# A hybrid attention and RWKV-7 trunk: head norms, rotary turn and forget gates moved from a stage of their own into the RWKV scan, and a new order of work in the forgetting attention

## The reference, cut to what matters

```python
def _hybrid_layer(x, pos, ...):
    h = _rmsnorm(x, norm_g)
    proj = h @ w_in
    (fq, fk, fv, ff, fg, r_pre, rg, sq, sk, sv, sg, cb, cc, cx, cg) = _split(proj, IN_COLS)
    y_fox = _fox_attention(_heads(fq), _heads(fk), _heads(fv), ff, fox_b_f, fox_q_norm, fox_k_norm)
    y_rwkv = _rwkv7_time_mix(r_pre, ...)
    y_swa = _swa_attention(_heads(sq), _heads(sk), _heads(sv), swa_sinks, swa_q_norm, swa_k_norm, pos)
    y_conv = _short_conv(cb, cc, cx, conv_w)
    mixed = jnp.concatenate([y_fox * silu(fg), y_rwkv * silu(rg), y_swa * silu(sg), y_conv * silu(cg)], axis=-1)
    return x + mixed @ w_out

def _fox_attention(q, k, v, f_logit, b_f, q_norm, k_norm):
    q, k = _rmsnorm(q, q_norm), _rmsnorm(k, k_norm)
    log_f = jax.nn.log_sigmoid((f_logit + b_f).astype(jnp.float32))
    Ft = jnp.cumsum(log_f, axis=1)
    # score = q.k * scale + F[query] - F[key], causal, softmax, times v

def _swa_attention(q, k, v, sinks, q_norm, k_norm, pos):
    q = _rope(_rmsnorm(q, q_norm), pos)
    k = _rope(_rmsnorm(k, k_norm), pos)
    # sliding window with sinks
```

## Time and profile before

| | us |
|---|---|
| median of 3 runs | 3686.85 (3685.52 to 3697.97) |
| profiled execution | 3691.14 |
| its span, first to last instruction | 3689.3 |
| PE busy | 3284.0 (89%) |
| DVE busy | 1552.2 (42%) |
| ACT busy | 1009.4 (27%) |
| POOL busy | 545.5 (15%) |
| mean granted PE clock | 0.916 of full |

### The profile page before, as it was taken

How to read it: one execution, slowest core, us unless ns; L and a number is a source line. 1 busy time by engine, 2 the same in 40 slices (tenths; PEclk the granted TensorE clock), 3 DMA queues, 4 the chain that set the end, 5 groups by cost and what they waited for, 6 DMA issues and landing times. The chain is left out here.

```text
span 3689.3 us, 62205 instructions
## 1 busy us (share of the span) xinstructions
PE 3284.0 (89%) x24708; PEld 2331.3 (63%) x24708; DVE 1552.2 (42%) x2258; ACT 1009.4 (27%) x1876; POOL 545.5 (15%) x304
## 2 busy tenths in 40 slices
PE   6979989999997688959979799899999976889599
PEld 4868767777774344437748687677777743444387
DVE  4127622222223565557441376222222235655575
ACT  4014312222223134333240143122222231343332
POOL 4100000000000112332241000000000001122322
PEclk9989999999998578979979899899999985788799
DMA  3225422222223310066332254222222233100663
GB/s 118 74 70 174 142 74 66 80 66 65 64 66 120 116 29 18 9 187 209 120 110 74 70 174 144 73 64 80 68 65 64 66 120 116 29 18 9 187 203 123
DMA packets 357723, 343.29 MB, mean 93 GB/s; under 512 B 95388, under 2 KB 290972, under 8 KB 353592
## 3 DMA queue, kind: packets, MB, share of 16 engines
q1 hardware_dynamic: 288520, 298.53, 25.5%
q10 hardware_dynamic: 68928, 40.93, 4.2%
HBM read 208.46 MB, written 130.91 MB: 92 GB/s over the span
## 5 line engine op out<-in xcount | busy, mean ns | idle before, releaser
L124 PE MATMUL rs_acc<-h_hi,rs_w_hi 128*128 128x512 f32 x1024 | 428.4, 418 | 0.0
L128 PE MATMUL rs_acc<-h_lo,rs_w_hi 128*128 128x512 f32 x1024 | 417.8, 408 | 0.0
L130 PE MATMUL rs_acc<-h_hi,rs_w_lo 128*128 128x512 f32 x1024 | 414.5, 405 | 0.0
L110 POOL TENSOR_TENSOR rs_w_lo<-rs_raw,rs_w_hi 128x1024 fp32r<-128x1024 f32 x32 | 76.3, 2386 | 1235.8 <-POOLq L109 1235.8
L124 PE MATMUL rp_acc<-h_hi,rp_w_hi 128*128 128x512 f32 x512 | 206.0, 402 | 41.7 <-PEq L121 41.7
L1372 ACT ACTIVATE fx_prob<-fx_ST 128x512 f32<-128x512 f32 (+3 forms) x320 | 157.2, 531 | 290.7 <-PE fx_ST L1242 150.8
L1658 PE MATMUL so_acc<-so_wo_hi,so_m_hi 128*128 128x512 f32 x512 | 209.3, 409 | 29.9 <-POOL so_m_lo L1580 25.2
L124 PEld LDWEIGHTS rs_acc<-h_hi,rs_w_hi 128*128 128x128 f32 x1024 | 192.2, 188 | 55.1 <-issue 16.5
L130 PEld LDWEIGHTS rs_acc<-h_hi,rs_w_lo 128*128 128x128 f32 x1024 | 192.6, 188 | 43.2
L128 PEld LDWEIGHTS rs_acc<-h_lo,rs_w_hi 128*128 128x128 f32 x1024 | 192.7, 188 | 36.7
L124 PE MATMUL pj_acc<-h_hi,pj_w_hi 128*128 128x512 f32 (+1 forms) x512 | 207.4, 405 | 5.3 <-PEq L121 5.3
(11 more groups left out here) (256 smaller groups left out, 6006.6 us busy)
## 6 DMA issues: line engine op xcount, KB each, us to landing
projT<-rs_stage SPq DMA_DIRECT2D x128, 256.0 KB, 2.1
pj_xb<-x SPq DMA_DIRECT2D x32, 512.0 KB, 3.3
projT<-rp_stage SPq DMA_DIRECT2D x64, 256.0 KB, 3.1
rs_raw<-w_in ACTq DMA_DIRECT2D x32, 512.0 KB
rs_nat<-rw SPq DMA_DIRECT2D x128, 128.0 KB, 2.4
so_stage<-x SPq DMA_DIRECT2D x64, 256.0 KB, 2.9
rp_pre<-projT SPq DMA_DIRECT2D x16, 899.5 KB, 8.3
projT<-pj_stage SPq DMA_DIRECT2D x56, 256.0 KB, 2.0
```

What stands on the lines that cost most here:

```text
L110: self.nc.gpsimd.tensor_tensor(self.w_lo[q][:, :, 0:m], self.raw[:, :, 0:m], self.w_hi[q][:, :, 0:m].bitcast(F32), ALU.subtract).then_inc( ...
L124: ins = M(acc, self.w_hi[q][:, k, 0:m], self.h_hi[:, k, cols], start=(k == 0), stop=False)
L128: M(acc, self.w_hi[q][:, k, 0:m], self.h_lo[:, k, cols], start=False, stop=False)
L130: ins = M(acc, self.w_lo[q][:, k, 0:m], self.h_hi[:, k, cols], start=False, stop=(k == KC - 1))
```

## The change

The head norm stage is dropped. Its work is cut into 56 units (seven blocks by eight ranges of 256 tokens), four in each of the first 14 tiles of the scan. A unit's squares are made by ACT, summed by head with one matmul on PE (`bones`, float32, 256 columns), the inverse root is taken by ACT (`factor`: Ln, then Exp), and POOL multiplies (`scale`). The 32 units of the forgetting attention come first (tiles 0 to 7); the 24 units with the turn follow (tiles 8 to 13): they also need the rows with halves of heads swapped, which SP loads by four transfers, and a block of cosines and sines. Loads and stores of the units go into SP's order between the stores of the projection (`beside`). The gates are made in tiles 0 to 7, 256 tokens each. `bt`, `kt` and `nat` of the scan lose their second buffer, so that the loads of tile `t+1` wait for `nb_free`, and the swapped rows and the cosines (`qp`, `cs`) have one buffer only.

In `phase_fox` the plan is paced: one or two `s` after each `m` (3 for 2 up to the 24th, then 19 for 20) regardless of the round, with seven of the second round's and first round's ahead of the first `m`; `r` is cut into four pieces; both heads' maxima go through one turn of four transposes in place of two of four; the evacuation `o` moves from DVE to ACT; `prob` has four buffers in place of three.

```diff
-        phase_head_norm(nc, l, projT, par, consts, rope, fa)
...
-        bt, kt = ([P.sb(f"{n}{e}", [128, NH, 64]) for e in two] for n in ("bt", "kt"))
-        nat = [P.sb(f"nat{e}", [128, 4, 2, 128]) for e in two]
+        bt, kt = P.sb("bt", [128, NH, 64]), P.sb("kt", [128, NH, 64])
+        nat = P.sb("nat", [128, 4, 2, 128])
...
+            sp.dma_start(bones[:], consts[:, 256:384]).then_inc(s["c_in"], 16)
+            sp.dma_start(gain[:], lay(par, l)[:, C_GN:C_GN + 7]).then_inc(s["c_in"], 16)
+            for a in range(0, 128, 32):
+                sp.dma_start(gainp[a ^ 32:(a ^ 32) + 32, :], lay(par, l)[a:a + 32, C_GN + 4:C_GN + 7]).then_inc(s["c_in"], 16)
+            sp.dma_start(bf[:], lay(par, l)[0:NH, C_BF - 1:C_BF + 1]).then_inc(s["c_in"], 16)
+
+            def load_norm(u):
+                e, (r, b) = u % 2, norms[u]
+                row, cols = row_of[r], slice(PAD + b * UB, PAD + (b + 1) * UB)
+                if u > 1:
+                    sp.wait_ge(q_st[e], 16 * (u // 2))
+                sp.dma_start(qx[e][:], projT[row:row + 128, cols]).then_inc(q_in[e], 16)
+                if turned(u):
+                    sp.wait_ge(s["q_out"], u)
...
+                    for a in range(0, 128, 32):
+                        sp.dma_start(qp[a ^ 32:(a ^ 32) + 32, :], projT[row + a:row + a + 32, cols]).then_inc(q_in[e], 16)
+                    sp.dma_start(cs[:], rope.rearrange("p (k t) -> p k t", k=2)[:, :, b * UB:(b + 1) * UB]).then_inc(q_in[e], 16)
+
+            def store_norm(u):
+                e, (r, b) = u % 2, norms[u]
+                sp.wait_ge(s["q_out"], u + 1)
+                sp.dma_start(projT[row_of[r]:row_of[r] + 128, PAD + b * UB:PAD + (b + 1) * UB], qx[e][:]).then_inc(q_st[e], 16)
...
+            def beside(t, b):
+                u = UT * t + b
+                if u < NU:
+                    store_norm(u)
+                    if b == 2 and t < NF:
+                        store_gates(t)
+                        if t + 1 < NF:
+                            load_gates(t + 1)
+                    if u + 2 < NU:
+                        load_norm(u + 2)
...
                     J.sp_store(sp, row, b)
+                    for i in ((0, 1), (2,), (3,), ())[b]:
+                        beside(t, i)
...
+            def scale(u):
+                e, r = u % 2, norms[u][0]
+                pool.wait_ge(s["q_sq"], u + 1)
+                G.tensor_scalar(qx[e][:], qx[e][:], gain[:, r:r + 1], None, ALU.mult)
+                if turned(u):
+                    G.tensor_scalar(qp[:], qp[:], gainp[:, r - 4:r - 3], None, ALU.mult)
+                pool.drain()
+                pool.wait_ge(s["q_fac"], u + 1)
+                G.tensor_tensor(qx[e][:], qx[e][:], qr[:], ALU.mult)
+                if turned(u):
+                    G.tensor_tensor(qp[:], qp[:], qr[:], ALU.mult)
+                    pool.drain()
+                    G.tensor_tensor(qx[e][:], qx[e][:], cs[:, 0, :], ALU.mult)
+                    G.tensor_tensor(qp[:], qp[:], cs[:, 1, :], ALU.mult)
+                    pool.drain()
+                    G.tensor_tensor(qx[e][:], qx[e][:], qp[:], ALU.add)
+                pool.drain().then_inc(s["q_out"], 1)
...
+            for t in range(NT):
...
+                for i, u in enumerate(here(t)):
...
+                    if i == 1 and t + 1 < NT:
+                        J.pool_weights(pool, (t + 1) % 2)
+                    scale(u)
...
+            def norm_sum(t, i):
+                u = UT * t + i
+                if u < NU:
+                    pe.wait_ge(s["q_sq"], u + 1)
+                    if u > 0:
+                        pe.wait_ge(s["q_fac"], u)
+                    M(bk[:, 5, UB:2 * UB], bones[:], qs[:], start=True, stop=True).then_inc(s["q_sum"], 1)
...
                 fill("p2")
+                norm_sum(t, 0)
...
                 fill("s5")
+                norm_sum(t, 1)
...
                     fill(f2)
+                    if f2 == "s7":
+                        norm_sum(t, 2)
...
                 fill("g")
+                norm_sum(t, 3)
...
+            def square(t, i):
+                u = UT * t + i
+                if u < NU:
+                    act.wait_ge(q_in[u % 2], loads[u])
+                    if u > 0:
+                        act.wait_ge(s["q_sum"], u)
+                    A(qs[:], qx[u % 2][:], ACT.Square).then_inc(s["q_sq"], 1)
...
                 evac("s3")
+                factor(t, 0)
...
                 evac("s4")
+                square(t, 1)
                 evac("s5")
...
                     evac(f1)
+                    factor(t, 1 if f1 == "s6" else 2)
+                    if f1 == "s6":
+                        square(t, 2)
                     evac(f2)
                 evac("wz")
+                square(t, 3)
                 evac("g")
+                factor(t, 3)
```

In `square`, `loads[u]` counts all transfers of a unit, for a turned one the six of its rows, its swapped rows and its cosines. In `phase_fox` the new part of the plan is:

```diff
-        NP = 3
+        NP = 4
...
-        LS = P.sb("LS", [128, 2 * QT, KX])
+        LS = P.sb("LS", [128, QT, KX])
...
+            for R in range(NR):
+                for j in range(keys[R % NQ]):
+                    turned(nm)
                     order.append(("m", R, j))
...
+                    goal = len(stat[0]) + 3 + min(nm, 24) * 3 // 2 + max(0, nm - 24) * 19 // 20
...
-                    for h in two:
-                        pe.wait_ge(s["lt_free"], lt_n[k, R, h] - 1)
-                        for j in range(QT):
-                            ins = Tr(LT[0:KX, j * 128:(j + 1) * 128], LS[:, QT * h + j, :], ident[:])
-                        ins.then_inc(s["lt_rdy"], 1)
+                    pe.wait_ge(s["lt_free"], lt_n[k, R] - 1)
+                    for j in range(QT):
+                        ins = Tr(LT[0:KX, j * 128:(j + 1) * 128], LS[:, j, :], ident[:])
+                    ins.then_inc(s["lt_rdy"], 1)
...
+                if k == "o":
+                    act.wait_ge(s["pv_done"], last[R])
...
+                    A(yo[:, R % 2], O[:], ACT.Copy).then_inc(s["o_free"], 1)
```

More of the change, by code:

```diff
@@ L594, in phase_rwkv_scan, with turned, here @@
         bk = P.ps("bk", [128, 6, 512])
+        UB = 256
+        bones = P.sb("bones", [128, 128])
+        qx = [P.sb(f"qx{e}", [128, UB]) for e in two]
+        qp, qs, qr = (P.sb(n, [128, UB]) for n in ("qp", "qs", "qr"))
+        cs = P.sb("cs", [128, 2, UB])
+        gain, gainp, eps = P.sb("gain", [128, 7]), P.sb("gainp", [128, 3]), P.sb("eps", [128, 1])
+        bf, one, carry = P.sb("bf", [NH, 2]), P.sb("one", [NH, 1]), P.sb("carry", [NH, 1])
+        ff, fg, fc = qp[0:NH, :], cs[0:NH, 0, :], cs[0:NH, 1, :]
+        norms = [(r, b) for r in range(4) for b in range(T // UB)] + [(4 + r, b) for r in range(3) for b in range(T // UB)]
+        row_of = [0, 128, 256, 384, R_SQ, R_SQ + 128, R_SK]
+        UT = 4
+        NU, NF = len(norms), T // UB
+        def turned(u):
+            return norms[u][0] > 3
+        def here(t):
+            return range(UT * t, min(UT * (t + 1), NU))
+        loads = [sum(96 if turned(i) else 16 for i in range(u % 2, u + 1, 2)) for u in range(NU)]
         J = Projector(P, nc, l, w_in, h_hi, h_lo, projT)
@@ L732, in body @@
                     take(pe, s[rdy])
+                    if c and here(t):
+                        pe.wait_ge(s["q_fac"], here(t)[-1] + 1)
                     a = (2, 0)[c]
@@ new lines, in plan, with ahead @@
+            turns, order, done, ns, nm = [], [], 0, 0, 0
+            total = sum(len(stat[R % NQ]) for R in range(NR))
+            def ahead(goal):
+                nonlocal done, ns
+                while done < len(beside) and (ns < goal or beside[done][0] == "x"):
+                    order.append(beside[done])
+                    ns += beside[done][0] == "s"
+                    if beside[done][0] == "x":
+                        turns.append((nm + 1, ("l", beside[done][1], 0)))
+                    done += 1
@@ L1099, in plan @@
+                    for r in range(1, NR):
+                        if nm >= sum(keys[i % NQ] for i in range(r)) - 2:
+                            goal = max(goal, sum(len(stat[i % NQ]) for i in range(r + 1)))
+                    ahead(min(total, goal))
             return order + [("o", NR - 1, 0), ("u", NR - 1, 0)]
@@ L1103, in phase_fox @@
         for k, R, x in order:
-            for h in (two if k == "l" else (0,) if k in "vu" else ()):
-                lt_n[k, R, h] = len(lt_n) + 1
+            if k in "lvu":
+                lt_n[k, R] = len(lt_n) + 1
         tiles = [(R, j) for R in range(NR) for j in range(keys[R % NQ])]
```

350 lines of the change are left out of this document (155 added, 195 removed).

## The result

The changed kernel takes 3738.11 us (median of 4 runs, 3735.56 to 3747.57) against 3688.83 before on the same chip: a ratio of 1.0134, 95% interval [1.0108, 1.0161]. It is slower by 1.3%. I had said 3647, a range of 3560 to 3728, and a chance of 0.17 for slower: wrong in direction, and outside the range. The profiled execution took 3735.56 (span 3733.8).

A forecast was written before the change was run, and what follows sets the result against it. Scan bound by PE's stream, norms by latencies, attention by waits and low-clock matmuls. From 3691: -220 stage removed, +8 start, +48 plain tiles, +204 turned tiles, -80 attention = 3651, as a median 3647; range 3560 to 3728.

The forecast's parts named there:

- Plain tiles: Scan tiles 0 to 7: sums 1.8 us plus PE standing 1.2 at the third unit's late square; +48 in all.
- Turned tiles: Scan tiles 8 to 13: PE's stands, sums and lower clock add 17.0 us a tile, +204 in all.
- Step 2: Turned tile: SP, held until POOL finishes, issues five transfers, landed 18.6; unit 1's square waits, PE stands 3.6 us.
- Steps 3 and 4: Turned tile: POOL's work and SP's queue with twelve loads land unit 2's transfers at 33.9; PE stands 10.2 us.
- Step 5: Turned tile, unit 3: the loop from square to square takes some 12 us, PE's work about 11; PE stands 1.
- the clock's term of 0.4: Turned tile: PE restarting at the lower level after a long stand loses 0.4 us a tile.
- POOL beside DVE: Scan: DVE's four two-input SBUF operations stand where POOL is idle, cost nothing; +24 us if that cover is gone.
- (b): Attention: pacing removes three quarters of PE's 20.6 us of waits for DVE's maxima, 15 us a layer.
- (c): Attention: evacuation on ACT removes up to 8.5 us of waiting, less what ACT's copy adds: 5 us a layer.
- (a): Attention: one turn of maxima in place of two saves four transposes and one wait, 9 us a layer.
- (d): Attention: steadier work gives back part of the time at the lower clock, 18 us a layer, bounds 0 and 45.
- rival for slower: Chance 0.17: turned units' loop taking 24 us a tile gives 3731, or an attention that gives nothing leads to 3727.

The follow-up runs named there:

- the run with the values alone: Changed kernel, with only the next round's values in the attention turned earlier, two maxima tiles ahead of the reduction: 3723.62 us, ratio 1.0094.
- the late turn: Changed kernel, attention's turn of the maxima one matmul tile later, next round's values turned ahead of the last two maxima tiles: 3678.16 us, ratio 0.9959.

## Why the prediction was wrong, point by point

**Stage removed, -220; start, +8.** The stage is gone, and so are its 220 us. DVE's first fill of the scan came at 468.55 in place of 464.43, and 1.3 of that was there at the stage before: 2.8 a layer, not 4.

**Plain tiles, +48.** 45.0 a tile in layer 0, 44.9 as the mean of both, where I said 44.65: +52. PE stood 7.8 us in eight tiles at the doubtful third sum (1.0 each, said 1.2). Right.

**Turned tiles, +204.** The mechanism was right to the place, in the tile shown: ACT's longest idle ends at the cosines, PE's stands were 4.0, 9.1 and 0.8 where I had 3.6, 10.2 and 1. The size was not: 20.95 a tile, 251 in all, 47 more. Count in the same clock, from the tile's start. Step 2: landed 18.9, said 18.6. Steps 3 and 4: the third square began at 34.95, its transfers said to land at 33.9. **Step 5 failed**: from that square to the next I took 12 us, it was 14.1, because POOL's scalings took 0.92 each where I had 0.5 estimated, the landing behind the last issue 2.8 where the earlier trace rows have 2.4 (for a quarter of the bytes of the cosines), and the factor stands behind `xn`, ready 5.0 us after the square began:

```profile
L740 POOL TENSOR_SCALAR rs_qx<-rs_qx,rs_gain 128x256 f32<-128x256 f32 x24 | 22.2, 923 | 152.0 <-ACT rs_qs L999 150.7 <-issue 1.3
L742 POOL TENSOR_SCALAR rs_qp<-rs_qp,rs_gainp 128x256 f32<-128x256 f32 x24 | 22.1, 922 | 0.0
L745 POOL TENSOR_TENSOR rs_qx<-rs_qx,rs_qr 128x256 f32<-128x256 f32 x24 | 17.6, 732 | 29.6 <-ACT rs_qr L1009 27.8 <-issue 0.9
```

Set against the terms of my sum the miss looks different, and a reader should know both views. PE's stands were 13.9 a tile where the sum has 14.8, its four sums cost 1.9 where it has 1.8 (PE is 43.6 us busy in a plain tile and was 41.7 before), and **the clock's term of 0.4 is the mis-sized one**: the tiles ran at 0.89, and PE was 4.3 us longer busy in the tile shown (47.9 against 43.6). That work filled time in which PE would have stood: between the end of its third stand and its place for the fourth sum it took 13.3 us where I had 11, beside a loop that was 14.1 where I had 12. So the third stand of 0.8, said 1, is luck: two errors met. The run with PE kept busy decides which of the two sets the tile, since the loop takes 13.4 at the fuller clock too and the tile stays. It also shows that the loop is not free of the clock: there the factor was ready 3.6 us after the square in place of 5.0, while the issue of the cosines took 1.21 us in place of 0.57.

**POOL beside DVE, 0.** DVE was busy 68.05 us in the six turned tiles, 11.34 each, as in the tile without units (11.35): no operation of DVE got longer. Right.

**The attention, -80.** It gave 43 in the traces, of which the new plan alone gave 17 (in its own run behind the norm stage; 20 by the medians). (b) 12.5 of 15. (c) all 9.1 where I took 5. **(a) failed**: I priced the single turn by what it removes, and not by what its place in the order makes it wait for. In the old plan the values were turned at the start of a round; in the new one they are turned behind the reduction, in the later rounds ahead of the turn of the maxima and through the same bank, and their copy on DVE must be awaited. And since PE no longer stands for the maxima themselves, it comes to the turn sooner than DVE to the reduction (argued from the 23.4 us of the run with the values alone). Together 20.6 us in place of 8.0. Not foreseen: the wait at the start of the stage fell from 18.0 to 12.7, which the move of the norms gave. **(d), the clock, failed too**: PE's busy time fell 17.4 in layer 0 and 3.4 in layer 1, but 6.1 and 5.6 of that are the 32 turns that are gone and belong to (a). By the clock PE got 11 and lost 2, where I took 18 a layer, and the 11 is the favourable end of what this stage shows. I had treated the clock as a gift of steadier work; the late turn shows that it is tied to the pauses, term (a) again.

Together: 47 from the turned tiles, 37 from the attention, 4 from the plain tiles, 2 back at the start: 86, and the profiled execution was 84.5 above my sum. Neither rival for slower came: its point of 22 us a turned tile was not reached, and the attention did gain. Both terms were wrong at once in the same direction, a case to which I had given hardly any chance.

## What to carry to other kernels

Where a helper engine's queue holds waits, follow one turn of the loop through every queue it passes, and put long blocks of issues inside a wait that the queue has anyway: here twelve loads of 0.6 us were worth 78 us. An instruction should wait for the data that it reads and nothing else, and costly units should be spread among cheap ones: with all six tiles full of turned units a tile took 62.6 us, with two of them in each tile and both waits mended 45.4, where a plain tile took 44.9. When a plan is reordered, price each step by what it then waits for, and count with a pause of PE the slower work that can follow it, unless another chain is as long. And before a few us of a stage whose clock varies are put down to a cause, look at the same stage in other kernels.

## What the runs showed of the hardware

POOL's operation with one input and a scalar per partition took longer than its addition of two tensors, 923 ns against 732 for 128x256, and hardly less (840 to 930 ns) for 4x256. A pause of PE of 5.4 us was followed by 7.4 us at the 1.2 GHz level. The attention of the same kernel ran at 0.84 in layer 0 and 0.79 in layer 1 with waits that agree within 1 us, and took 15 us longer. The clock behind one and the same pause differed: behind the wait of 1.2 us for the values in layer 0 the next 9.9 us of work ran at full clock, behind its twin in layer 1 at the lower level.

```profile
1440.10:1450.00 9.90, 9.86 (x46) 5.06 (x46) 6.03 (x6) 5.33 (x10) 4.67 (x2) 1.00 0.38 108
3306.60:3316.50 9.90, 9.87 (x26) 4.89 (x27) 2.88 (x3) 3.45 (x6) 2.35 (x1) 0.50 0.36 108
```

The same time of work holds 46 matmuls in the one and 26 in the other. Why the clock fell behind one of them alone is open. With the pauses shortened both layers were at 0.87.
